# Accumulating the adaLN blocks of a group in one PSUM bank, in a two-layer diffusion step on one Trainium2 core

## What is computed

```python
def adaln(cvec, w, b):
    m = jax.nn.silu(cvec) @ w + b          # w: 1024 x 6144 for each layer
    m = m.reshape(cvec.shape[:-1] + (1, 6, D_MODEL))
    return [m[..., i, :] for i in range(6)]   # shift, scale, gate of mixer and of experts

m_ctx = adaln(c_ctx, w_mod[l], b_mod[l]);  m_lat = adaln(c, w_mod[l], b_mod[l])
h = modulate(rms_norm(x, norm1_g[l]), m[0], m[1])     # x * (1 + scale) + shift
```

## Time and profile before

| What | us |
|---|---|
| three runs | 1335.37, 1341.05, 1341.48 |
| median of the runs | 1341.05 |
| the profiled execution | 1336.44 |
| its span, first to last instruction | 1334.8 |
| TensorE busy | 1087.7 (81%) |
| ScalarE busy | 381.7 (29%) |
| VectorE busy | 319.8 (24%) |
| GpSimd busy | 118.3 (9%) |
| mean granted clock of TensorE | 0.937 |

### The profile page before, as it was taken

How to read it: one execution, slowest core, us unless ns; L and a number is a source line. 1 busy time by engine, 2 the same in 40 slices (tenths; PEclk the granted TensorE clock), 3 DMA queues, 4 the chain that set the end, 5 groups by cost and what they waited for, 6 DMA issues and landing times.

```text
span 1334.8 us, 16405 instructions
## 1 busy us (share of the span) xinstructions
PE 1087.7 (81%) x6064; PEld 617.9 (46%) x6065; DVE 319.8 (24%) x869; ACT 381.7 (29%) x729; POOL 118.3 (9%) x201
## 2 busy tenths in 40 slices
PE   4899999889898299777997279899893897799991
PEld 1444545446454155444664044455551454365651
DVE  3332132433443200000000054555524000000003
ACT  4221101432323122122232046554632222222220
POOL 0000002000100211000110210000001010011112
PEclk9999999999999789888999689999996899999995
DMA  9644417641925749999999802221072699999984
GB/s 368 285 189 189 189 63 305 270 189 64 379 88 228 314 155 398 394 401 399 387 386 397 314 25 109 88 80 63 1 309 114 262 389 397 406 391 385 383 335 149
DMA packets 35287, 341.58 MB, mean 256 GB/s; under 512 B 4912, under 2 KB 6064, under 8 KB 17328
## 3 DMA queue, kind: packets, MB, share of 16 engines
q1 hardware_dynamic: 21744, 295.97, 56.0%
q0 software_dynamic: 13504, 45.10, 9.4%
HBM read 313.00 MB, written 28.05 MB: 256 GB/s over the span
## 4 chain that ended last, share of the span: by engine, by line
PE 57%; DMA 24%; DVE 7%; ACT 5%; issue 4%; POOL 2%; POOLq 0%; DVEq 0%; SPq 0%; ACTq 0%
PE bank L1602 12%; PE bank L1531 10%; DMA arena<-in_moe 10%; PE bank L1523 8%; DMA ring<-in_moe 6%; PE bank L1797 6%; PE bank L1617 5%; DMA arena<-slots 3%; DMA ring<-in_proj 2%; PE bank L1494 2%; PE bank L1508 2%; PE bank L1719 2%; DMA arena<-slots,arena 1%; POOL slots L622 1%; PE bank L1500 1%
## 5 line engine op out<-in xcount | busy, mean ns | idle before, releaser
L1531 PE MATMUL bank<-ring,hT 128*128 128x512 f32 x384 | 169.8, 597 | 5.5 <-ACT hT L732 4.3
L1602 PE MATMUL bank<-arena 128*64 128x256 f32 x1216 | 143.4, 392 | 27.2 <-DMA arena<-in_moe 25.4
L1602 PE MATMUL bank<-ring,arena 128*64 128x256 f32 x1216 | 146.1, 398 | 23.6 <-DMA ring<-in_moe 20.2
L1291 DVE TENSOR_TENSOR arena<-bank,arena 128x256 f32<-128x256 f32 x38 | 16.1, 425 | 545.2 <-PE bank L1602 545.2
L1602 PEld LDWEIGHTS bank<-arena 128*64 128x64 f32 x1216 | 100.5, 141 | 75.3 <-DMA arena<-in_moe 23.4
L1602 PEld LDWEIGHTS bank<-ring,arena 128*64 128x64 f32 x1216 | 101.3, 144 | 72.1 <-DMA ring<-in_moe 22.3
L1531 PEld LDWEIGHTS bank<-ring,hT 128*128 128x128 f32 x384 | 72.3, 192 | 91.7 <-issue 88.6
L1523 PE MATMUL bank<-hT,ring 128*128 128x384 f32 x320 | 108.0, 498 | 4.5 <-ACT hT L732 2.5
L785 ACT ACTIVATE arena<-bank 128x256 f32<-128x256 f32 x80 | 30.6, 383 | 234.3 <-PE bank L1578 234.0
L1797 PE MATMUL bank<-cT,ring 128*128 128x384 f32 x256 | 84.6, 487 | 0.0
L1523 PEld LDWEIGHTS bank<-hT,ring 128*128 128x128 f32 x320 | 61.9, 195 | 48.7 <-issue 6.5
(11 more groups left out here) (268 smaller groups left out, 1134.9 us busy)
## 6 DMA issues: line engine op xcount, KB each, us to landing
ring<-in_moe SPq DMA_DIRECT2D x48, 2048.0 KB, 21.0
arena<-in_moe SPq DMA_DIRECT2D x48, 2048.0 KB, 22.4
ring<-in_proj SPq DMA_DIRECT2D x41, 2048.0 KB, 10.2
arena<-slots POOLq DMA_DIRECT2D x42, 256.0 KB, 8.8
slots<-arena POOLq DMA_DIRECT2D x76, 128.0 KB, 7.4
slots<-blank POOLq DMA_DIRECT2D x1, 7680.0 KB, 38.3
arena<-in_hyconst SPq DMA_DIRECT2D x1, 2432.0 KB, 14.7
xT<-in_x SPq DMA_DIRECT2D x1, 1536.0 KB, 11.5
```

Of the source, the lines that this page charges most:

```text
L1531: ins = mm(ps[:, :], src[:, k, P * i : P * i + P], w[:, k, :], start=k == 0, stop=k == KD - 1)
L1602: ins = mm(psum[kind][CAP * half : CAP * half + CAP, 0:FHALF], mo["hS"][:, k, :], wk[:, k, FHALF * half : FHALF * half + FHALF], start=k = ...
```

## The change

The 24 adaLN blocks form three groups: blocks 0 to 3, blocks 4 to 11 and blocks 12 to 23. All blocks of a group are accumulated in bank 7. For this `condT` is widened from 32 to 62 columns with the conditioning in the columns 30 and 31 and zeros elsewhere; the block at place a of its group takes the window of 32 columns that puts the conditioning at columns 2a and 2a + 1, so that it adds its results to rows of its own and zeros to all others. A block is then eight matmuls and nothing else. A group is finished by one new step, `turn_mods`: one copy by ScalarE, four transposes, and on VectorE four reductions, one addition of the bias and the multiplications by the gain. The step of the first group stands ahead of `apply1`; that of the second stands behind the second tile of the projection ff, and block 11 has moved to behind the first tile of ff; that of the third stands behind block 23 in the routing stage. The norms wait for whole groups. In layer 0 the other steps take turns over seven banks instead of eight; the names `ada` and `adt` of single blocks leave the plan. A ring slot that held an adaLN block is released by the block's last matmul, as before. The order of `STREAM` is unchanged.

```diff
+MOD_GROUPS = [(0, 0, MOD_FIRST), (0, MOD_FIRST, MOD_BLOCKS), (1, 0, MOD_BLOCKS)]
+MOD_BANK = 7
+WINDOW = 2 * (BLK - 1)
...
-    ("hf1",), ("sum1",), MODS[0], ("hf2",), *MODS[1:MOD_FIRST], ("apply1",),
+    ("hf1",), ("sum1",), MODS[0], ("hf2",), *MODS[1:MOD_FIRST], ("turn_mods", 0), ("apply1",),
...
-    *project("ff"), *MODS[11:13],
+    *project("ff")[:1], MODS[11], *project("ff")[1:2], ("turn_mods", 1), *project("ff")[2:], MODS[12],
...
-LATE_MODS = MODS[22:]
+LATE_MODS = MODS[22:] + [("turn_mods", 2)]
...
-            self.next = (bank + 1) % BANKS
+            self.next = (bank + 1) % self.turning
...
@@ ScalarE
-            def modulation(layer, b):
-                if mods_done[0] >= 2:
-                    full(act, "adt", *MOD_ALL[mods_done[0] - 2])
-                full(act, "ada", layer, b)
-                nc.scalar.activation(ada[:, mods_done[0] % 2, :], bank("ada", layer, b)[:, :], ACT.Copy).then_inc(free_of("ada", layer, b), 1)
+            def turn_mods(g):
+                layer, _, end = MOD_GROUPS[g]
+                if g:
+                    full(act, "adt", g - 1)
+                act.wait_ge(mod_done, MOD_ALL.index((layer, end - 1)) + 1)
+                nc.scalar.activation(ada[:, :], psum[MOD_BANK][:, :], ACT.Copy).then_inc(mod_copied, 1)
...
@@ VectorE
+            def turn_mods(g):
+                layer, first, end = MOD_GROUPS[g]
+                n = end - first
+                full(dve, "adt", g)
+                chunks = mod[:, layer, 4 * first : 4 * end, :].rearrange("p (b m) s -> p m b s", m=4)
+                turned = bank("adt", g)[:, :].rearrange("p (m g b s) -> p m b s g", m=4, g=4, s=2)
+                for m in range(4):
+                    ins = V.tensor_reduce(chunks[:, m], turned[:, m, 0:n], AX_X, ALU.add)
...
@@ TensorE
+                g = group_of(layer, b)
+                at_block = b - MOD_GROUPS[g][1]
+                if g and at_block == 0:
+                    pe.wait_ge(mod_copied, g)
+                cond = condT[:, :, BLK - 2 - 2 * at_block : 2 * BLK - 2 - 2 * at_block]
                 for k in range(KD):
                     rows = slice(BLK * (k % 4), BLK * (k % 4) + BLK)
-                    ins = mm(ps[rows, :], condT[:, k, :], w[:, k, :], start=k < 4, stop=k >= 4)
-                ins.then_inc(full_of("ada", layer, b), 1)
-                n = MOD_ALL.index((layer, b))
-                freed(pe, "ada", layer, b)
-                ps = open_bank("adt", layer, b)
+                    ins = mm(psum[MOD_BANK][rows, :], cond[:, k, :], w[:, k, :], start=at_block == 0 and k < 4,
+                             stop=b == MOD_GROUPS[g][2] - 1 and k >= 4)
+                ins.then_inc(mod_done, 1)
+
+            def turn_mods(g):
+                pe.wait_ge(mod_copied, g + 1)
+                ps = open_bank("adt", g)
                 for m in range(4):
-                    ins = nc.tensor.transpose(ps[:, P * m : P * m + P], ada[:, n % 2, P * m : P * m + P], ident)
-                ins.then_inc(full_of("adt", layer, b), 1)
+                    ins = nc.tensor.transpose(ps[:, P * m : P * m + P], ada[:, P * m : P * m + P], ident)
+                ins.then_inc(full_of("adt", g), 1)
```

More of the change, by code:

```diff
@@ L74, with group_of @@
 MODS = [("mod", layer, b) for layer in range(DEPTH) for b in range(MOD_BLOCKS)]
+MOD_GROUPS = [(0, 0, MOD_FIRST), (0, MOD_FIRST, MOD_BLOCKS), (1, 0, MOD_BLOCKS)]
+MOD_BANK = 7
+WINDOW = 2 * (BLK - 1)
+def group_of(layer, b):
+    return next(g for g, (of, first, end) in enumerate(MOD_GROUPS) if of == layer and first <= b < end)
 EVEN_COLUMN = {"q": 0, "ff": 1, "fb": 2, "v": 3, "g": 4, "hy0": 5, "hy1": 6, "hy2": 7}
@@ L439, in mods_needed @@
         def mods_needed(layer, which):
-            return MOD_ALL.index((layer, MOD_FIRST - 1 if which == 0 else 5 * D // HALF - 1)) + 1
+            return group_of(layer, MOD_FIRST - 1 if which == 0 else 5 * D // HALF - 1) + 1
         def keeps(u):
@@ L773, in experts @@
                 if layer == 0:
-                    for step in LATE_MODS:
-                        modulation(*step[1:])
+                    turn_mods(2)
                 act.wait_ge(route_max, 2 * layer + 1)
@@ L998, in _ @@
             V = nc.vector
[L1000 to L1011, removed]
-                    link(biased)
-                    k = slice(chunk - KD, chunk - KD + 4)
-                    gain = (n1, n2)[which][:, layer, k].unsqueeze(2).to_broadcast([P, 4, 2])
-                    V.scalar_tensor_tensor(gs[:, layer, which, k, :], mod[:, layer, 4 * b : 4 * b + 4, :], 1.0, gain,
-                                           ALU.add, ALU.mult).then_inc(mod_ready, 1)
-                else:
-                    biased.then_inc(mod_ready, 1)
-                dve.wait_ge(mod_ready, MOD_ALL.index((layer, b)) + 1)
@@ new lines, in turn_mods @@
+            def turn_mods(g):
[6 more added lines that the diff above has]
+                    ins = V.tensor_reduce(chunks[:, m], turned[:, m, 0:n], AX_X, ALU.add)
+                ins.then_inc(free_of("adt", g), 1)
+                freed(dve, "adt", g)
+                b_mod = pr("b_mod").rearrange("p (l n) -> p l n", l=DEPTH)[:, layer, 4 * first : 4 * end]
+                now = mod[:, layer, 4 * first : 4 * end, :]
+                link(V.tensor_tensor(now, now, b_mod.unsqueeze(2).to_broadcast([P, 4 * n, 2]), ALU.add))
+                for which in range(2):
+                    scales = 4 * (6 * which + 2)
+                    if 4 * first <= scales < 4 * end:
+                        gain = (n1, n2)[which][:, layer, :].unsqueeze(2).to_broadcast([P, KD, 2])
+                        ins = V.scalar_tensor_tensor(gs[:, layer, which, :, :], mod[:, layer, scales : scales + KD, :], 1.0, gain,
+                                                     ALU.add, ALU.mult)
+                ins.then_inc(mod_ready, 1)
+                dve.wait_ge(mod_ready, g + 1)
@@ L1555, in experts @@
                 if layer == 0:
-                    for step in LATE_MODS:
+                    for step in MODS[22:]:
                         modulation(*step[1:])
+                    turn_mods(2)
                 pe.wait_ge(assigned, layer + 1)
```

43 lines of the change are left out of this document (24 added, 19 removed).

## The result

| | before | after |
|---|---|---|
| median of the runs timed side by side, 11 each | 1340.44 us | 1329.03 us (1325.28 to 1334.9) |
| ratio after to before, 95% interval | 1 | 0.9926 (0.9909 to 0.9942) |
| span of the profiled execution | 1334.8 us | 1327.4 us |
| TensorE, mean granted clock in it | 0.937 | 0.922 |

The change is faster by 0.74%, about 9.9 us (7.8 to 12.2) by the ratio; the medians stand 11.4 apart. The forecast was 1325, in a range that holds the measurement, but its sum of -16.4 us is 1.7 times what came. So the question for the experiments is where some 7 us went.

The account below looks back on a forecast made before the run. TensorE's work and waits, with weight loads, were taken to bound the kernel until 470 us. Terms summed to -16.4 us (bounds -20.6 and -3.5), taking the median 1341.05 to 1324.6: forecast 1325 us, range 1316 to 1335.

Parts of the forecast that it names:

- Blocks 10, 13, 14: Removed waits and transposes beside ready work: gains of 1.4, 5.1 (3.4 if the clock falls) and 1.4 us.
- Blocks 0 to 3 and 4, 5: Up to hy0 and step G: gains of 2.7 us (0.8 with a fallen clock) and 1.4 us (at least 0).
- Blocks 6 to 9: Inside the load waits of hy2 and q: removal buys nothing, idling slows q; loss 1.7 us, bounds 0 and 1.7.
- ff, the turn, fb: ff ends 3.9 us later, fb starts where it did, the clock costs 1.0: loss 1.0 us, bounds -0.9 and 5.6.
- fb stands first in its queue, so the loads behind it should not hold it: At fb's load: the argument against a much later fb although block 13's load is queued at once behind it.
- slower rival: fb's load, issued 3.9 us later beside the blanking write, takes up to 31.2 us: 1348 us, chance 0.05.
- Blocks 15 to 21: Up to the output projection: loads pass by 361.3 us, so the output starts there at the earliest; gain 6.0 us.
- Blocks 22, 23: In the routing stage, with four reductions, bias and gains on VectorE: gain 1.1 us, bounds 1.4 and -0.1.
- One to one to the end: Behind the routing stage: its shift, 16 us earlier, passes whole through the experts to the end.
- the waits give most of it back: Rival: fb's load takes 12.26 us again and each new wait costs clock; sum -9 to -3.5, 1335 us, chance 0.16.
- Nothing is pinned: Rival: loads land earlier than the rows say, so 34 us are gained: 1307 us, chance 0.06.
- no effect: Rival: the experts' weight stream, not the routing stage, sets the end of layer 0: 1341 us, chance 0.05.

Follow-up runs that it names:

- the later turn: The changed kernel with block 11, turn 1 and block 12 moved back behind the whole of ff: 1327.13 us, ratio to before 0.9907.
- the turns at 13 and 14: The changed kernel with copy, wait and four transposes put back behind each of blocks 13 and 14: 1333.7 us, ratio to before 0.9954.
- the sixteen zeros: The changed kernel with four zero matmuls ahead of each of hy2, q, fb and block 18: 1321.4 us, ratio to before 0.9852.
- the held write: The changed kernel with GpSimd's blanking write of 7680 KB held back until fb's block has landed: 1323.78 us, ratio to before 0.9875.
- at 15 to 21: The changed kernel with copy, wait and transposes put back behind each of blocks 15 to 21: 1333.8 us, ratio to before 0.995.

## Why the prediction was right, and where its sum was not

**Blocks 10, 13, 14** were right to 0.2 us: -1.42, -4.96 and -1.24 against -1.4, -5.1 and -1.4. TensorE has ready work on both sides of these blocks, so what is removed is gained. Put back, blocks 13 and 14 cost 4.4 us of the 6.2.

**Blocks 0 to 3 and 4, 5** look right (-2.84 and -1.07) but the first partly by chance: 1.10 us of it is the first norm's sixteen matmuls, 8.16 before and 7.06 after, which the change doesn't touch (6.93 to 8.30 in the other profiles of kernels with the change). The step itself brought 1.7, between the 2.7 and the 0.8 that I gave for a fallen clock. The clock did fall: block 3's 1.92 us became 3.21. It doesn't in every execution: in the profiles of the later turn, of the turns at 13 and 14 and of the sixteen zeros block 3 keeps its 1.97 us behind the same wait, and hy0 pays instead, 23.6 to 23.8 us against 22.3 before. From the norm's end to hy0's end the gain is 1.0 to 1.5 us in all nine profiles that have nothing put ahead of block 3. So the 2.7 was too much by about half.

**Blocks 6 to 9: the term was mis-sized, +3.9 for +1.7 in this execution.** That they lie inside the waits, that hy2 and q wait as before (7.47 and 7.56 us against 7.65 and 7.37), and that the idling costs the clock was right. I charged it at q alone, as if hy2 had paid already, with 1.7 as the upper bound. Both paid, and more: hy2 1.3 and q 2.6 over the kernel before. In six profiles without turns at blocks 6 to 9 (the changed kernel twice, the later turn, the held write, turns at 13 and 14 and at 15 to 21) hy2 takes 22.33 to 23.87 us and q 22.60 to 23.55; in the two with turns, and with the zeros, both take 20.9. The six fall into two kinds. In the changed kernel twice and with the held write the two take about 23.8 and 23.5. In the other three they take 22.3 to 22.6 and 22.6, which is the forecast's 1.7 at q and nothing at hy2; here the later turn:

```profile
115.24 22.61 PE bank L1545 x64
...
145.43 22.60 PE bank L1545 x64
```

The waits are alike in both kinds, 3.8 to 4.3 us, and what decides between them is open. So the bound, which was the one loss that the kernel before happened to show (22.61 against 20.91), is right in half of the executions seen, and in the others the loss goes up to 3.0. The four turns that I counted as worth nothing were worth 3.3 to 5.5 us to keep in the profiles, 3.4 in the mean of the runs.

The Trainium skill ("TensorE: Matmul & The Clock Gate", section "Loop structure matters more than you think"), weighed in the prediction as speaking against this change at block 3, q and fb, was right at q and fb, and at block 3 in six of nine profiles; the runs add hy2 and block 18.

**ff, the turn, fb: mis-sized, +4.4 for +1.0.** ff's part was right: from its start to its end 24.5 us, 3.9 more than 20.6. fb's load was taken as 8.2 us and took 10.34, so fb came 2.0 us later instead of where it was; its tile took 9.39 instead of 7.13, 2.3 us where I had 1.0 for the clock. Two reasons of the sum fall. The blanking write had not 0.3 MB left beside fb but 1.08; before, it had moved 2.32 MB beside fb and not 1.9, and 0.4 were still to come when fb had landed. And "fb stands first in its queue, so the loads behind it should not hold it" is wrong by 1.0 MB: without the write the load still takes 8.62. That these bytes are what lengthens it was not tried alone. Block 11, now done before ff ends, lets block 13's load go 0.4 us behind fb's, and block 12 lets block 14's go 2.0 us behind it, where before they went 1.9 and 6.7 us behind. This is the slower rival's mechanism, in a small size: 10.34 us, far from the 24.1 from which it decides.

**Blocks 15 to 21: mis-sized, -3.7 for -6.0.** I took the loads' end, 361.3, as fixed in time, since block 15 ended no earlier. That contradicts my own sum, whose terms up to there put block 15 at 9.3 us earlier; and a gain up to a fixed end could not have been added to them. Block 15 did end earlier, by 3.2 us, and the loads moved with it; the output began at 360.72 without a wait. That this is near 361.3 is luck: in the profile with the sixteen zeros it began at 353.07. What is fixed is the length: from block 15 to the output 31.4 us in the changed kernel, and 30.8 to 30.9 in the five profiles of kernels that reach block 15 earlier (with the turns at 6 to 9, and with zeros). Zeros ahead of block 18 don't shorten it further; in all five the output waits 1.2 us for its load. So the loads pass in 30.8, not in 28.8, and 4.3 us is the most that these seven turns can bring. I had read the end of the transfers from a DMA share that falls to 0.72, which doesn't say that the last load has landed.

**Blocks 22, 23** brought 1.9 instead of 1.1, with the bounds at 1.4 and -0.1: better than I thought possible, by 0.5. VectorE's timeline shows part of it: the four reductions took 0.75 us together where I had 1.08, and bias and gains 0.6 instead of 0.7.

**One to one to the end** held as far as the spread of that stretch lets one see: -9.2 at the experts (-9.0 in the second profile), -9.9 by the ratio.

Of the rivals, "the waits give most of it back" (1335) named the right mechanism at the right places. It gives -9 to -3.5, and the measurement, -9.9, lies just outside its better end. "Nothing is pinned" and "no effect" are out by the landmarks.

The best kernel of the study is the changed one with sixteen zero matmuls, 1321.4 us, ratio 0.9852. The plainer way, with the same 20.9 us at hy2 and q, is to keep the turns of blocks 6 to 9 apart (0.9903 and 0.9912 in two sets of runs); it leaves fb's loss where it is.

## What to carry to other kernels

Before you remove work from the engine that carries the chain, sort its places: beside ready work the removal is worth its whole time, inside a wait for a transfer it is worth nothing, and where the wait then grows by some 3 us it can cost, because what follows may run at half clock. Whether it does can differ between executions of the same steps, so look at more than one profile before you price it. When a release moves earlier than its neighbours', look at what it lets into the queue behind a transfer that matters. And read a bound on loads as a length from the release that starts them, not as a fixed moment.

## What the runs showed of the hardware

- TensorE's clock: behind a wait for hy2's load of about 4 us without other work the granted clock was 0.50 and the 64 matmuls took 23.9 us (22.3 to 22.6 in three of six such profiles); with two copies, two sets of four turns and their short waits in the same gap it stayed 1.00 and they took 20.9. The kernel before, with a last gap of 1.16 us at hy2 and 0.87 at q, had 22.61 and 20.91. What made the difference between these two is open. Block 3, behind an empty wait of 3.2 to 3.5 us, took 1.9 us in three profiles and 2.7 to 3.4 in six.
- A load that is first in its queue doesn't move alone: while 2.1 MB of fb were under way, 1.0 MB of the loads issued behind it moved too, and it took 8.62 us with no other queue at work, where loads ahead of hy2 and q took about 7.4.
- A zero matmul of 128x128 by 128x512 takes 0.86 us (3.44 for four, eight records); an adaLN block's eight matmuls of 128x32 by 128x512 take 1.9 us, 0.24 each. They go to four row positions of the bank, 32 rows each; that this is what makes them shorter was not tried alone.
- Setting aside one of eight PSUM banks in layer 0 cost nothing: ratio 1.001 (0.9987 to 1.0032).
